# A pool layer and two attention layers on one core: context tiles in one step, and bands of 8 columns as tiles

## What is computed

```python
# first attention layer (mixer_a): windowed, four key heads, rotary, a sink logit per head
mask = (jnp.abs(qi[:, None] - kj[None, :]) <= A_WINDOW) & ...     # A_WINDOW = 128
p = softmax([s_lat (masked), s_ctx, s_sink])                      # s * HEAD_DIM ** -0.5
o = p_lat @ v + p_ctx @ v_ctx
oc = ctx_attention(qc, kc, vc, sink)                              # 256 context queries see 256 context keys
y = (o * silu(g)) @ w_out ; yc = (oc * silu(gc)) @ w_out

# second attention layer (mixer_b): a neighbourhood of 8 rows x 16 columns, clamped at the edges
s = q . k * scale + rel_bias[head, row_idx, col_idx]              # rel_bias: 15 x 31 a head
s = where(col_mask, s, NEG_INF)
p = softmax([s, s_ctx]) ; o = p_lat @ v + p_ctx @ v_ctx
y = (o * silu(g)) @ w_out
```

## Time and profile before

| | us |
|---|---|
| median of three runs (2025.32 to 2027.76) | 2025.38 |
| the profiled execution | 2027.67 |
| its span | 2025.8 |
| PE busy | 1973.2 |
| DVE / ACT / POOL busy | 1074.9 / 825.6 / 829.3 |
| first attention | about 695 to 1187 |
| second attention | about 1338 to 1926 |

### The profile page before, as it was taken

The page is one execution under the profiler, slowest core; times in us unless marked ns, Lnnn a source line. Parts: engine busy times, 40 slices in busy tenths (PEclk is TensorE's granted clock), DMA queues, the critical chain, the costliest instruction groups (busy, mean ns, idle before and its releaser), DMA issues.

```text
span 2025.8 us, 36948 instructions
## 1 busy us (share of the span) xinstructions
PE 1973.2 (97%) x14892; PEld 1637.8 (81%) x14892; DVE 1074.9 (53%) x2229; ACT 825.6 (41%) x1639; POOL 829.3 (41%) x623
## 2 busy tenths in 40 slices
PE   7999999999999999999999999999999999999996
PEld 6888888888887888888888788778888888888785
DVE  5556556766855665556666733734334433434625
ACT  4110110110126566566677610745554555555601
POOL 3433333323345712222122625555445345344846
PEclk9999999999999999999999999999999999999998
DMA  4432322332221401110011423221111111111333
GB/s 160 135 99 85 107 95 83 107 102 84 94 93 65 157 12 45 35 35 22 25 35 36 135 91 115 76 90 53 43 53 53 42 53 53 43 52 53 110 120 135
DMA packets 51063, 156.02 MB, mean 77 GB/s; under 512 B 5584, under 2 KB 9296, under 8 KB 50768
## 3 DMA queue, kind: packets, MB, share of 16 engines
q1 hardware_dynamic: 49888, 152.40, 22.8%
q10 hardware_dynamic: 1008, 1.27, 0.2%
HBM read 132.94 MB, written 20.71 MB: 76 GB/s over the span
## 4 chain that ended last, share of the span: by engine, by line
PE 64%; DVE 4%; issue 2%; ACT 2%; POOL 1%; DMA 1%; DVEq 0%; SPq 0%; POOLq 0%; ACTq 0%
PE psum L924 16%; PE psum L926 14%; PE psum L925 14%; PE psum L1113 8%; PE psum L1060 6%; PE psum L1076 5%; PE psum L933 1%; POOL w_lo L738 1%; DVE prob_t L1838 1%; DMA w_raw<-weights_in 1%; ACT logits L1394 0%; DVE logits L1816 0%; PE psum L1087 0%; DVE u_lo L1693 0%; ACT u_tmp L1324 0%
## 5 line engine op out<-in xcount | busy, mean ns | idle before, releaser
L924 PE MATMUL psum<-u_hi,w_hi 128*128 128x512 f32 (+1 forms) x1440 | 544.8, 378 | 2.6 <-DVE u_lo L1693 2.6
L925 PE MATMUL psum<-u_lo,w_hi 128*128 128x512 f32 (+1 forms) x1440 | 525.4, 365 | 0.0
L926 PE MATMUL psum<-u_hi,w_lo 128*128 128x512 f32 (+1 forms) x1440 | 525.3, 365 | 0.0
L736 POOL CAST w_hi<-w_raw 128x1024 fp32r<-128x1024 f32 x140 | 157.4, 1124 | 818.8 <-DMA w_raw<-weights_in 818.8
L738 POOL TENSOR_TENSOR w_lo<-w_raw,w_hi 128x1024 fp32r<-128x1024 f32 x140 | 347.8, 2484 | 11.2
L924 PEld LDWEIGHTS psum<-u_hi,w_hi 128*128 128x128 f32 x1440 | 272.5, 189 | 54.9 <-DVE u_lo L1693 4.4
L926 PEld LDWEIGHTS psum<-u_hi,w_lo 128*128 128x128 f32 x1440 | 272.5, 189 | 44.9
L925 PEld LDWEIGHTS psum<-u_lo,w_hi 128*128 128x128 f32 x1440 | 273.1, 190 | 38.7
L1394 ACT ACTIVATE logits<-logits,neg_max 128x640 f32<-128x640 f32 (+2 forms) x288 | 226.0, 785 | 71.5 <-DVE neg_max L1816 70.0
L1403 ACT ACTIVATE logits<-logits,row_rec 128x640 f32<-128x640 f32 (+1 forms) x288 | 218.0, 770 | 0.0
L1417 ACT ACTIVATE prob_t<-psum 128x320 f32<-128x320 f32 (+1 forms) x288 | 118.7, 412 | 235.5 <-PE psum L1076 235.4
(11 more groups left out here) (164 smaller groups left out, 3037.3 us busy)
## 6 DMA issues: line engine op xcount, KB each, us to landing
w_raw<-weights_in SPq DMA_DIRECT2D x140, 512.0 KB, 3.5
w_ada<-w_ada_in SPq DMA_DIRECT2D x48, 512.0 KB, 3.5
residual<-act_buf SPq DMA_DIRECT2D x4, 2048.0 KB, 7.4
tab<-bias_tab_in SPq DMA_DIRECT2D x16, 496.5 KB
res<-residual SPq DMA_DIRECT2D x26, 256.0 KB, 3.4
y_all<-staged SPq DMA_DIRECT2D x24, 256.0 KB, 4.7
act_buf<-x_t_in SPq DMA_DIRECT2D x8, 512.0 KB, 13.3
staged<-a_y SPq DMA_DIRECT2D x6, 640.0 KB, 3.0
```

What stands on the lines that cost most here:

```text
L736: pool.tensor_copy(w_hi[:, slot, :], w_raw[:, slot, :]).then_inc(w_hi_done, 1)
L924: pe.matmul(out, wh, xh, start=first, stop=False)
L925: pe.matmul(out, wh, xl, start=False, stop=False)
L926: return pe.matmul(out, wl, xh, start=False, stop=last)
```

## The change

**First layer.** Tiles 8 and 9 become one step (`CTX_TILE`), so a pair has 9. It has the same matmuls, on two groups of 256 logits in one row, each with a maximum, sum and reciprocal of its own (`neg_max`, `row_sum`, `row_rec` get a second column), and one gating of 256 columns. The pair's projections are cut in 9 parts with the first three larger by 22% (`early`), the last pair's parts are cut anew, and the steps of the rotary (`rope_times`) come one earlier for most q and k.

**Second layer.** A tile is a band of 8 columns by 16 rows (`BAND`). q, k and v are stored in band order (`in_bands`, runs of 8 floats), so that the keys of a tile are three neighbouring bands (two for the first and the last) and contiguous. Values need 10 tiles in place of 18 and are turned in five turns. The gate chunks stay in row order but each covers half of the columns of all rows (`half_columns`, runs of 32 floats of the modulated rows, on PE's moving operand too). Three biases serve all 8 tiles: one for each edge and one for the six inner bands, which is built in the step of the pair before. The table is 31 x 31, scaled by POOL after it is loaded, and the scale of q is applied in the logits. One mask (`b_mask`) is loaded. Some loads of gated rows wait for parts of the last gate chunk (`late_part`) in place of all of it.

**Buffers** from `w_ada` on begin at a multiple of 128 bytes.

```diff
-KEY_COL = (0, 8, 24, 32)
-COL_TYPE = (0, 1, 1, 2)
-KEY_ROWS, KEY_COLS = 12, 32
-LAT_KEYS = KEY_ROWS * KEY_COLS
+BAND = P // ROWS
+LAT_KEYS = 3 * P
 KEYS = LAT_KEYS + C
 KEY_TILES = KEYS // P
-TAB_R, TAB_C = 23, 63
-TAB_RUN = TAB_R * TAB_C - (7 * TAB_C + 15)
-TAB_ROWS = 16
-B_BUILDS = 6
-LAST_BIAS_USE = ((1, 6), (1, 7), (0, 0), (0, 2), (0, 3), (0, 4))
-TILES = (S // P + C // P, S // P)
+TAB = 2 * ROWS - 1
+TAB_RUN = (ROWS - 1) * TAB + ROWS + BAND
+BIAS_FIRST = (0, -1, -1)
+MASK_AT = (0, 2 * P, 5 * P)
+B_BUILDS = 3
+LAST_BIAS_USE = (0, 6, 7)
+CTX_TILE = S // P
+TILES = (CTX_TILE + 1, S // P)
...
-V_TILE, V_TURNS, V_TILES = (0, 3), (2, 3), (S // P + C // P, 18)
+V_TILE, V_TURNS, V_TILES = (0, 3), (2, 2), (S // P + C // P, S // P + C // P)
...
+EARLY_PARTS = 3
+def in_parts(row, parts, early=0.0):
     cost = [(c, k, c.tn * 0.00134 if c.kind != "t" else 0.11) for c in row for k in range(c.steps)]
     total, past = sum(t for _, _, t in cost), 0.0
     cut = [[] for _ in range(parts)]
     for c, k, t in cost:
-        part = cut[min(parts - 1, int((past + t / 2) / total * parts))]
+        done = (past + t / 2) / total
+        part = cut[min(parts - 1, int(done / (1 + early) * parts) if done < (1 + early) * EARLY_PARTS / parts else
+                       int(EARLY_PARTS + (done - (1 + early) * EARLY_PARTS / parts) / (1 - (1 + early) * EARLY_PARTS / parts) * (parts - EARLY_PARTS)))]
...
-    return parts + ([[(b0, 0, 5)], [(b0, 5, 7), (b1, 0, 7)], [(third, 0, 4)], [(third, 4, 7)]],
+    return parts + ([[(b0, 0, 6)], [(b0, 6, 7), (b1, 0, 7), (third, 0, 2)], [(third, 2, 7)]],
...
-PARTS = tuple([in_parts(row, TILES[layer]) for row in STAGES[layer][1:-1]] + [in_parts(STAGES[layer][-1][:-1], TILES[layer])]
+PARTS = tuple([in_parts(row, TILES[layer], (0.22, 0.0)[layer]) for row in STAGES[layer][1:-1] + [STAGES[layer][-1][:-1]]]
...
-                times[c.kind, c.pair] = tuple(min(n + d, last) for d in (1, 3, 4))
+                times[c.kind, c.pair] = tuple(min(n + d, TILES[0] - (2 if c.kind == "q" else 1)) for d in (1, 3, 4))
...
+    at[0] = (at[0] + 127) // 128 * 128
...
+    def in_bands(rows, n):
+        return rows[:, 0:S].rearrange("p (b r c) -> p r b c", c=BAND, r=ROWS)[:, n * ROWS // 2:(n + 1) * ROWS // 2]
...
+    def half_columns(rows, n):
+        return rows[:, 0:S].rearrange("p (r c) -> p r c", c=GRID)[:, :, n * GRID // 2:(n + 1) * GRID // 2]
...
-            sp.wait_ge(pj_done, chunks)
             sp.wait_ge(y_stored, 16 * STAGED * (layer + 1))
+            if chunks is not None:
+                sp.wait_ge(pj_done, chunks)
             for k in range(STAGED):
+                if chunks is None and k % 3 == 0:
+                    sp.wait_ge(late_part, k // 3 + 1)
...
-        load_y(1, y_loaded, Y_FIRST[1], BO_CHUNK - 1)
+        load_y(1, y_loaded, Y_FIRST[1], None)
...
-            half, kind, slot = b // 3, b % 3, b % 2
-            d = -4 * half
-            e = -8 * kind
-            r0, c0 = 11 - d, 31 - e
+            lo = 0 if b == 1 else P
             for h in range(2):
-                back, tile = LAST_BIAS_USE[b]
-                pool.wait_ge(logit_done, (j - back) * B_STEPS + (STEP0[1] + 2 * tile + h + 1))
-                src = tab[h][:, :].rearrange("p (r c) -> p r c", c=TAB_C)
-                src = src[:, r0 - KEY_ROWS + 1:r0 + 1, c0 - KEY_COLS + 1:c0 + 1][:, ::-1, ::-1]
-                dst = bias[:, h, slot, 0:LAT_KEYS].rearrange("p (r c) -> p r c", c=KEY_COLS)
-                cm = col_mask[:, kind, :].rearrange("p (a c) -> p a c", a=1).to_broadcast([P, KEY_ROWS, KEY_COLS])
-                rm = row_mask[:, half, :].rearrange("p (r a) -> p r a", a=1).to_broadcast([P, KEY_ROWS, KEY_COLS])
-                step(pool.tensor_tensor(dst, src, cm, ALU.add))
-                pool.tensor_tensor(dst, dst, rm, ALU.add).then_inc(bias_ready, 1)
+                if j:
+                    pool.wait_ge(logit_done, STEP0[1] + (j - 1) * B_STEPS + 2 * LAST_BIAS_USE[b] + h + 1)
+                dst = bias[:, h, b, lo:LAT_KEYS].rearrange("p (g r c) -> p g r c", r=ROWS, c=BAND)
+                mask = b_mask[:, MASK_AT[b]:MASK_AT[b] + LAT_KEYS - lo].rearrange("p (g r c) -> p g r c", r=ROWS, c=BAND)
+                for g in range((LAT_KEYS - lo) // P):
+                    at = (1 - BIAS_FIRST[b] - g) * BAND
+                    ins = pool.tensor_tensor(dst[:, g], tab[h][:, :, at:at + BAND][:, ::-1, ::-1], mask[:, g], ALU.add)
+                ins.then_inc(bias_ready, 1)
         def first_bias(j):
             pool.wait_ge(tab_loaded, (j + 1) * 32)
-            for b in range(2):
+            for h in range(2):
+                flat = tab[h].rearrange("p r c -> p (r c)")[:, 0:TAB_RUN]
+                step(pool.tensor_scalar(flat, flat, 1.0 / Q_SCALE, None, ALU.mult))
+            for b in range(1 if j else B_BUILDS):
                 bias_tile(j, b)
+        pool.wait_ge(mask_loaded, 32)
         first_bias(0)
         residuals(1, 1)
         for n in range(B_UNIT, B_UNIT + 4):
             split(n + W_SLOTS)
         for j in range(PAIRS):
             n, more = B_UNIT + 4 * (j + 1), j + 1 < PAIRS
-            bias_tile(j, 2)
             if more:
                 split(n + W_SLOTS)
-            if not more:
-                split_y(1, 0, 1)
-            bias_tile(j, 3)
-            if not more:
-                split_y(1, 2, 3, 4)
-            bias_tile(j, 4)
+            if j:
+                bias_tile(j, 2)
             if more:
                 split(n + 1 + W_SLOTS)
-            else:
-                split_y(1, 5, 6)
-                split_late(1, 0, 1, 2, 3)
-            bias_tile(j, 5)
-            if not more:
-                split_late(1, 4, 5, 6)
-                split(BO_UNIT + 2)
-            if more:
                 first_bias(j + 1)
                 split(n + 2 + W_SLOTS)
+                bias_tile(j + 1, 1)
                 if j + 2 < PAIRS:
                     split(n + 3 + W_SLOTS)
+            else:
+                split_y(1, *range(KT - 1))
+                split_late(1, *range(KT - 1))
+                split(BO_UNIT + 2)
...
+                        if layer == 1 and c.kind == "g":
+                            xs = half_columns(u_hi[:, k, :], c.n), half_columns(u_lo[:, k, :], c.n)
+                        else:
+                            xs = u_hi[:, k, c.t0:c.t0 + c.tn], u_lo[:, k, c.t0:c.t0 + c.tn]
+                        mm = product(out[:, 0:c.tn], (w_hi[:, slot, w], w_lo[:, slot, w]), xs, n == 0, n == c.steps - 1)
...
+            for i, (c, k0, n) in enumerate(key_span(t)[1]):
+                at, q0 = score_column(layer, t, c), (t + i if ctx_queries(layer, t) else t) * P
...
+                first, last, at = c == 0, c == len(tiles) - 1, 0
+                if ctx_queries(layer, t):
+                    first, last, at = c % 2 == 0, c % 2 == 1, c // 2 * P
...
+                if layer == 1:
+                    out, src = half_columns(y, c.n), src.rearrange("p (r c) -> p r c", c=GRID // 2)
...
-                act.activation(bk[c.pair % 2][0][:, span], src, ACT.Copy, scale=Q_SCALE).then_inc(b_hi_done, 1)
+                hi = bk[c.pair % 2][0]
+                if c.n < 2:
+                    ins = act.activation(in_bands(hi, c.n), by_rows(src), ACT.Copy)
+                else:
+                    ins = act.activation(hi[:, span], src, ACT.Copy)
+                ins.then_inc(b_hi_done, 1)
...
-                    for cb in range(4):
-                        dst = b_vt[:, cb * HALF + c.n * C:cb * HALF + (c.n + 1) * C].rearrange("p (r c) -> p r c", c=KEY_COLS)
-                        ins = act.activation(dst, src.rearrange("p (r c) -> p r c", c=GRID)[
-                            :, :, KEY_COL[cb]:KEY_COL[cb] + KEY_COLS], ACT.Copy)
+                    ins = act.activation(in_bands(b_vt, c.n), by_rows(src), ACT.Copy)
...
+            if ctx_queries(layer, t):
+                row = lg[:, c0 - 1:c0 + C]
+                act.activation(row, row, ACT.Exp, scale=-1.0, bias=neg_max[:, n, 1:2], accum_out=row_sum[:, n, 1:2])
+                c0 += C
...
+            if ctx_queries(layer, t):
+                pr = logits[n][:, c0 - 1:c0 + C - 1]
+                act.activation(pr, pr, ACT.Copy, scale=row_rec[:, n, 1:2])
+                c0 += C
...
+                if t == CTX_TILE:
+                    mid = c0 + C
+                    step(dve.tensor_copy(logits[n][:, mid - 1:mid], start))
+                    dve.wait_ge(score_done, s + 1)
+                    dve.tensor_tensor_reduce(logits[n][:, c0 - 1:mid - 1], ps_score[h][:, score_column(0, t, c0):score_column(0, t, mid)],
+                                             a_mask[:, m0:m0 + C], -1.0, start, ALU.add, ALU.min, neg_max[:, n, 1:2])
+                    c0 = mid
...
-                b = 3 * (t // 4) + COL_TYPE[t % 4]
-                start, add = NO_MAX, bias[:, h, b % 2, :]
+                b = 0 if t == 0 else 2 if t == TILES[1] - 1 else 1
+                start, add = NO_MAX, bias[:, h, b, c0:KEYS]
...
```

(14 more changed lines are left out.)

174 lines of the change are left out of this document (81 added, 93 removed).

## The result

| | before | after |
|---|---|---|
| median, us (lowest to highest, 4 runs each) | 2026.2 (2025.32 to 2027.76) | 2038.21 (2035.75 to 2040.95) |
| ratio | | 1.0059, 95% interval 1.0041 to 1.0076 |
| profiled execution (span) | 2027.67 (2025.8) | 2039.82 (2038.0) |
| start to the first scores of the first layer | 695.1 | 714.2 |
| from there to the first scores of the second | 643.7 | 640.7 |

The account below looks back on a forecast made before the run. PE was taken as the bound, busy 480.5 of 492 us and 583.1 of 588 in the two attentions. Savings of 15.5 (second layer) and 4.4 (first) make 19.9 off 2025.38: 2005.5 us, own forecast 2002 to 2009, range 1998 to 2013.

Parts of the forecast that it names:

- The rounding to 128 bytes: Buffer layout: rounding was said to move no buffer against a multiple of 128, counted at nothing.
- The strided operand at zero: Second layer's gate chunks: reading the moving operand in runs of 32 floats was counted at nothing.
- The rival: Gate chunks: the strided operand slows 384 matmuls; 52 ns more each would lose all 19.9 us; chance 0.04.
- second layer, a pair: Second attention: fewer score columns, transposes, outputs and value turns save 1.73 us a pair (1.5 to 2.0).
- second layer, pairs 0 and 6: Second attention: besides 1.73 a pair, 1.2 us saved at the layer's start and 1.1 by the bias in pair 6.
- first layer, pairs 1 and 2: First attention: the merged context step was to keep 1.1 us of saving in pair 1 and 1.3 in pair 2.
- first layer, pair 6: First attention: 2.6 us won, but waits of 2.3 to 2.9 for DVE and slower rotation; counted at zero.
- the logits' waits for POOL's bias: Second layer, mainly pair 6: one bias for six bands, built a pair ahead, gives 1.1 us back.
- The 10.6 for eight pairs: First attention: merging the two context tiles saves 1.3 us a pair, if nothing takes its place.
- the chain of the context step: First attention: ACT's copy ends at 7.5 us, PE arrives at 6.5; 0.9 to 1.0 us wait in pairs 0, 3, 4, 5.
- the first rival: First attention: ACT's and DVE's instructions lie earlier, so the layer gives 10.6 us or little less, total 1999; chance 0.18.
- the 0.6 that I had put there: First layer, pair 6: DVE's rotation slowed beside POOL (2.44 against 1.21 us), half the difference counted as cost.

Follow-up runs that it names:

- best: old_consts with the second layer's gate chunks of pairs 0 to 6 read and stored over 512 neighbouring columns, runs of 32 only in the last pair: 2005.28 us.
- cin_late: best without the two small mask transfers, and with the 1 MB of c_in issued by ACT only after the third tile of x has landed: 2005.63 us.
- old_consts: Changed kernel with the two removed small transfers back on ACT's queue, into 480 bytes, so the large buffers lie as in the kernel before: 2007.87 us.
- after_p384: Changed kernel with 384 bytes more ahead of w_ada, so the large buffers begin at the same byte as in the kernel before: 2014.3 us.

## Why the prediction was wrong, step by step

I had 2005.5; it became 2038.2. The sum of the two attention layers was near, and `best` came to 2005.3 with it. What failed was three edits that I had costed at nothing, or not looked at.

1. *"The rounding to 128 bytes moves no buffer against a multiple of 128, so nothing."* True, and beside the point. It was this line and the removed masks that moved the buffers by 384 bytes against the weights, and the pool layer with all else on PE got slower: 22 to 24 us of the whole, of which 14.3 lie outside the part of the program that I was looking at. I had bounded it from neither side; there was no row of before with another placing, and the text took that for a price of zero. An edit that moves buffers is an edit to every instruction that reads them, until a run shows otherwise.
2. *The strided operand at zero, by the 337 and 334 ns of two score matmuls*. The two rows were right, and the conclusion was not. They are mean durations, where the prediction itself reads costs from distances; but the distances of these score matmuls say the same (177 ns in runs, 175 without). They come in pairs of 64 partitions, and an operand of 512 columns over 128 partitions costs 13 ns more in the same runs. The rival had the mechanism, with 52 ns as its point of decision; the true price was a quarter of that, 4 to 5 us in all. Between "nothing" and "loses all" the sum should have had a bound.
3. *The transfers of two masks are not in the prediction's text at all.* Without them the 1 MB of `c_in` goes 1.05 us earlier (2.79 for 3.84) and the stretch of slow transfers comes 3 us earlier, and PE waited 3.8 us for x at the start: 4 to 6 us. `c_in` has only a part in it (`cin_late`).

With all three undone, 2038.2 becomes 2005.3; I was off by 32.7. With the steps undone the terms can be held against the profile of `old_consts` and `best`:

| term | forecast | measured |
|---|---|---|
| second layer, a pair | -1.73 | -1.64 (pair 1: 76.47 to 74.83, `best`), -1.1 with runs of 32 |
| second layer, pairs 0 and 6 | -2.9 and -2.8 | -3.3 and -2.8 (77.08 to 73.76, 72.86 to 70.07, `best`) |
| second layer, to the end | -15.0 (0.5 lie ahead) | -14.7 (687.0 to 672.3, `best`) |
| first layer, pairs 1 and 2 | -1.1 and -1.3 | -0.3 and -1.9 (68.65 to 68.40, 70.51 to 68.65) |
| first layer, pair 3 | -0.2 | -1.1 (58.68 to 57.58) |
| first layer, pairs 4 and 5 | -0.2 each | -0.7 and -0.9 (56.50 to 55.78, 56.61 to 55.71) |
| first layer, pair 6 | 0 | -0.5 (53.45 to 52.92) |
| first layer, pair 0 with all behind pair 6 | -1.9 | -0.9 (59.27 to 55.86, 220.0 to 222.5) |
| first layer, to the second | -4.9 (4.4 and the 0.5 above) | -6.3 (643.7 to 637.4) |

A pair is measured from its first scores to those of the next. Rows without a name are of `old_consts`.

The counts of the second layer held. Its edge band is as I reckoned it (timeline of `after_p384`: 0.87 us from the scores to the transposes):

```profile
1411.11 0.36 PE L1071 MATMUL psum<-bk_hi,bq_hi 64*128 64x256 f32 x2
...
1411.55 0.28 PE L1071 MATMUL psum<-bk_hi,bq_hi 64*128 64x256 f32 x2
...
1411.98 0.47 PE L1087 MATMUL psum<-ident,logits 64*128 64x64 f32 x8
```

and of the logits' waits for POOL's bias, 15.3 us in all before with the 4.00 of the earlier trace rows among them, the changed kernel has a single one of 0.4 us left.

In the first layer the sum came near over terms that mostly did not, so that `best` meets 2005.5 to 0.2 us is luck in part. (The 10.6 for eight pairs is also a slip: 8 x 1.3 is 10.4.) Its mechanism was the wrong size. I had the chain of the context step end one microsecond after PE. In pair 4 of the changed kernel its scores are held up a little and the transposes not at all:

```profile
1016.10 0.37 PE L1071 MATMUL psum<-ak_hi,aq_hi 64*128 64x256 f32 x2
...
1016.78 0.28 PE L1071 MATMUL psum<-ak_hi,aq_lo 64*128 64x256 f32 x2
1017.14 0.46 PE L1087 MATMUL psum<-ident,logits 64*128 64x64 f32 x8
...
1021.75 0.46 PE L1087 MATMUL psum<-ident,logits 64*128 64x64 f32 x8
1022.02 0.36 PE L1071 MATMUL psum<-ak_hi,aq_hi 64*128 64x256 f32 x2
...
1023.24 0.47 PE L1087 MATMUL psum<-ident,logits 64*128 64x64 f32 x8
```

The scores of the step take 1.04 us to the transposes where 0.87 is the least, those after them (from 1022.02) 1.22 where 0.87 would do. That is 0.2 and 0.3 of wait, and not 1.1 at the transposes. The three rows of ACT and DVE that count are these:

```profile
1019.97 0.50 ACT L1411 ACTIVATE logits<-logits,neg_max 128x257 f32<-128x257 f32 x1
...
1022.54 0.36 ACT L1439 ACTIVATE prob_t<-psum 128x256 f32<-128x256 f32 x1
```

```profile
1022.68 0.42 DVE L1870 COPY prob_t<-psum 128x256 f32<-128x256 f32 x1
```

Counted from 1016.10 as in the prediction, the last exponential ends at 4.4 and not 4.9, ACT's copy at 6.8 and not 7.5 (DVE's at 7.0), and PE, without the wait, would be there at 6.8 and not 6.5. So my sum of ten durations made the chain too long, and I had PE arrive too early. For pairs 3 to 5 the first rival ("the context step hides its chain", -1.3 a pair) was nearer than my forecast: they have -0.9 in the mean. For the layer as a whole, where it had -10.6, the forecast was nearer.

In pair 6 the mechanism came true in another place. DVE's split of the rotated q ends at 1130.93, and what waits for it is the scores of the next pair (the profile's releaser is only "issue"):

```profile
1128.85 0.46 PE L1087 MATMUL psum<-ident,logits 64*128 64x64 f32 x8
1131.03 0.39 PE L1071 MATMUL psum<-ak_hi,aq_hi 64*128 64x256 f32 x2 [1.72 <-issue]
```

1.9 us from where they could have begun; I had 2.3 to 2.9. POOL's splitting hardly overlapped the rotation's addition this time (in `old_consts` it took 1.29 us, against the 2.44 of the earlier trace rows), so the 0.6 that I had put there was not paid.

## What to carry to other kernels

When a change frees or rounds space ahead of large buffers, first write down where each operand lies before and after. A difference in an untouched stage is then looked for there, by the distance between starts, since the busy share (97% both times) doesn't show it. An edit gets the price zero only if a row of the *same* instruction form shows it; a near form gives a bound. And a removed transfer counts as an edit of everything behind it on its queue and of what the other queues move meanwhile.
